# Moving the values of an attention core by one item, joining its softmax guards, and reordering the norm ahead of two mixers

## The reference

```python
def rmsnorm(x, g):
    y = xf * lax.rsqrt(jnp.mean(xf * xf, axis=-1, keepdims=True) + EPS)
    return (y * g.astype(jnp.float32)).astype(x.dtype)

def attend_block(qb, keys, values, masks, sink):
    ...
    m = sink_f
    for s in scores:
        m = jnp.maximum(m, jnp.max(s, axis=-1))
    denom = jnp.exp(sink_f - m)
    for s, vp in zip(scores, values):
        p = jnp.exp(s - m[..., None])
        denom = denom + jnp.sum(p, axis=-1)
        out = out + jnp.einsum('bkgqs,bskd->bqkgd', p.astype(vp.dtype), vp).astype(jnp.float32)
    out = out / jnp.moveaxis(denom, -1, 1)[..., None]
    ...

def fourier_mix(h, w):
    f = jnp.fft.fft2(hg, axes=(1, 3), norm='ortho').real
    return f.reshape(B, L, D).astype(h.dtype) @ w
```

## Time and profile before

| | before |
|---|---|
| median of 3 runs | 2664.11 us (2659.36 to 2665.26) |
| the profiled execution | 2665.53 us, its span 2663.7 us |
| TensorE matmuls busy | 2573.9 us, 97% of the span |
| VectorE busy | 1984.8 us, 75% |
| ScalarE busy | 1299.1 us, 49% |
| GpSimd busy | 115.5 us, 4% |
| mean granted TensorE clock | 0.984 of full |
| attention core of layer 0 | about 143 to 275 us |
| norm and pooling mixer | about 814 to 862 us |
| norm and start of the Fourier mixer | about 1328 to 1357 us |
| attention core of layer 3 | about 2014 to 2132 us |

### The profile page before, as it was taken

The page is one execution under the profiler, slowest core; times in us unless marked ns, Lnnn a source line. Parts: engine busy times, 40 slices in busy tenths (PEclk is TensorE's granted clock), DMA queues, the critical chain, the costliest instruction groups (busy, mean ns, idle before and its releaser), DMA issues.

```text
span 2663.7 us, 43103 instructions
## 1 busy us (share of the span) xinstructions
PE 2573.9 (97%) x15856; PEld 2383.5 (89%) x15856; DVE 1984.8 (75%) x3736; ACT 1299.1 (49%) x2291; POOL 115.5 (4%) x146
## 2 busy tenths in 40 slices
PE   6989999999998999999989999999998999999999
PEld 4966899999998999999879999999997699999998
DVE  3777488888896888888855888888868946754772
ACT  3467365425524663355244662454347936633551
POOL 2000100000012000000101000000100010000000
PEclk9999899999998999999989999999999999999999
DMA  7224122433341334434302335334320012222222
GB/s 292 64 95 148 58 101 104 163 138 118 108 168 48 103 110 160 154 105 146 124 21 72 116 111 184 111 110 153 118 71 29 2 56 72 78 87 64 76 83 78
DMA packets 72274, 279.64 MB, mean 105 GB/s; under 512 B 7888, under 2 KB 11344, under 8 KB 68560
## 3 DMA queue, kind: packets, MB, share of 16 engines
q1 hardware_dynamic: 72144, 277.93, 30.5%
HBM read 274.75 MB, written 3.15 MB: 104 GB/s over the span
## 4 chain that ended last, share of the span: by engine, by line
PE 89%; DVE 7%; issue 2%; ACT 1%; DMA 1%; POOL 0%; SPq 0%; DVEq 0%; ACTq 0%
PE ps L575 20%; PE ps L573 16%; PE ps L574 16%; PE ps L576 15%; PE ps L577 11%; PE ps L792 2%; PE ps L777 2%; PE ps L761 1%; PE ps L634 1%; DVE h L1406 1%; PE ps L687 1%; DVE prob L1609 1%; DVE ada_w L1352 1%; PE ps L828 1%; PE ps L569 1%
## 5 line engine op out<-in xcount | busy, mean ns | idle before, releaser
L575 PE MATMUL ps<-h,w_hi 128*128 128x512 f32 x1768 | 700.5, 396 | 0.0
L573 PE MATMUL ps<-h,w_hi 128*128 128x386 f32 x1768 | 604.8, 342 | 8.2 <-DVE h L1406 4.9
L574 PE MATMUL ps<-h,w_hi 128*128 128x386 f32 x1768 | 602.9, 341 | 0.0
L576 PE MATMUL ps<-h,w_lo 128*128 128x386 f32 x1768 | 598.7, 339 | 0.0
L950 ACT ACTIVATE tail<-ps 128x256 f32<-128x256 f32 x281 | 108.3, 386 | 966.0 <-PE ps L577 965.4
L577 PE MATMUL ps<-h,w_lo 128*128 128x256 f32 x1768 | 503.4, 285 | 0.0
L577 PEld LDWEIGHTS ps<-h,w_lo 128*128 128x128 f32 x1768 | 333.7, 189 | 79.6
L1293 DVE TENSOR_TENSOR w_lo<-w_raw,w_hi 128x1024 fp32r<-128x1024 f32 (+1 forms) x288 | 377.4, 1311 | 4.9 <-ACT w_hi L945 1.7
L573 PEld LDWEIGHTS ps<-h,w_hi 128*128 128x128 f32 x1768 | 339.3, 192 | 11.3 <-DVE h L1406 7.2
L574 PEld LDWEIGHTS ps<-h,w_hi 128*128 128x128 f32 x1768 | 335.8, 190 | 0.0
L575 PEld LDWEIGHTS ps<-h,w_hi 128*128 128x128 f32 x1768 | 334.0, 189 | 0.0
(11 more groups left out here) (166 smaller groups left out, 3890.0 us busy)
## 6 DMA issues: line engine op xcount, KB each, us to landing
w_raw<-in_w_in SPq DMA_DIRECT2D x176, 512.0 KB, 3.6
w_raw<-in_w_out SPq DMA_DIRECT2D x64, 704.0 KB, 4.1
ada_w<-in_ada_t SPq DMA_DIRECT2D x42, 1024.0 KB, 6.3
row_w<-in_ada_t SPq DMA_DIRECT2D x60, 512.0 KB, 3.5
ada_w<-in_ada_w SPq DMA_DIRECT2D x18, 1024.0 KB, 5.0
w_raw<-in_w_qkv SPq DMA_DIRECT2D x24, 512.0 KB, 3.5
w_raw<-in_w_o SPq DMA_DIRECT2D x16, 512.0 KB, 3.5
first_w<-in_ada_w SPq DMA_DIRECT2D x6, 1024.0 KB, 14.3
```

The costliest lines, as they stand in the source:

```text
L573: pe.matmul(main, wh, b[:, 0, 0:MAIN], start=first, stop=False)
L574: pe.matmul(main, wh, b[:, 1, 0:MAIN], start=False, stop=False)
L575: pe.matmul(wide, wh, b[:, :, MAIN:NT], start=first, stop=last, skip_group_check=True)
L576: pe.matmul(main, wl, b[:, 0, 0:MAIN], start=False, stop=last)
```

## The change

It has four edits.

1. In the attention core, `values(w)` comes one iteration later on TensorE (`values(w-3)`), with `out_hi` and `out_lo`; `probT` gets a third buffer. The loops run one iteration longer.
2. `masked` runs both heads' mask passes, then forms both guards with two instructions over both heads (a product and a minimum) in place of one two-scalar instruction for each head. `max_made` counts items in place of heads, so `exps(w)` waits for both heads' guards.
3. Ahead of the pooling and Fourier mixers GpSimd doesn't add the last square. TensorE sums `sq_sum` with six squares added, then, in the same accumulation, the last square by itself.
4. Ahead of the Fourier mixer the tables are split behind the root: four between the inversion and the copy into `rstd`, six after the first four tiles.

```diff
@@ gpsimd
-                        pool.tensor_tensor(sq_sum[:], sq_sum[:], sq[kk % 2][:], ALU.add).then_inc(sq_added, 1)
+                        if kk == KT - 1 and explicit(layer, second):
+                            pool.sem_inc(sq_added, 1)
+                        else:
+                            pool.tensor_tensor(sq_sum[:], sq_sum[:], sq[kk % 2][:], ALU.add).then_inc(sq_added, 1)
@@ tensor
-                pe.wait_ge(sq_added, (KT - 1) * (m + 1))
+                lone = explicit(layer, second)
+                pe.wait_ge(sq_added, (KT - 1) * (m + 1) - lone)
...
-                block_sums(sq_sum, ones[:], 1).then_inc(sum_done, 1)
+                if not lone:
+                    block_sums(sq_sum, ones[:], 1).then_inc(sum_done, 1)
+                    return
+                block_sums(sq_sum, ones[:], 1, last=False)
+                pe.wait_ge(sq_added, (KT - 1) * (m + 1))
+                block_sums(sq[(KT - 1) % 2], ones[:], 1, first=False).then_inc(sum_done, 1)
...
-                            pe.wait_ge(max_made, 2 * (w - 1))
+                            pe.wait_ge(max_made, w - 1)
...
-                        if w - w0 >= 2:
-                            values(w - 2)
+                        if w - w0 >= 3:
+                            values(w - 3)
@@ scalar
+                        act.wait_ge(max_made, w + 1)
                         for hd in range(2):
                             st = stat[:, w % 2, hd, :]
-                            act.wait_ge(max_made, 2 * w + hd + 1)
...
-                        if w - w0 >= 2:
-                            act.wait_ge(o_done, w - 1)
+                        if w - w0 >= 3:
+                            act.wait_ge(o_done, w - 2)
...
-                        if w - w0 >= 2:
-                            out_hi(w - 2)
+                        if w - w0 >= 3:
+                            out_hi(w - 3)
...
+                    high_tables(range(4))
                     shifted(layer, range(4))
-                    high_tables(range(8, 10))
+                    high_tables(range(4, 10))
...
-                if layer + 1 < DEPTH and KINDS[layer + 1] == "fnet":
-                    act.wait_ge(unit_done, UNIT0[layer + 1])
-                    high_tables(range(8))
@@ vector
                 if m:
                     invert(r, 1)
+                if KINDS[layer] == "fnet" and not second:
+                    split_tables(range(4))
                 dve.wait_ge(inv_turned, r + 1)
...
-                if kind == "fnet":
-                    split_tables(range(8))
...
-                    split_tables(range(8, 10))
+                    split_tables(range(4, 10))
...
-                            dve.tensor_scalar(st[:, 1:2], st[:, 0:1], neg_scale[:, tile, nb, hd:hd + 1],
-                                              neg_sink[:, a, head:head + 1],
-                                              ALU.mult, ALU.min).then_inc(max_made, 1)
+                        st, head = stat[:, w % 2, :, :], 8 * ga + r
+                        if w - w0 < KT:
+                            dve.wait_ge(q_scaled, KT * a + tile + 1)
+                        own.link(dve.tensor_tensor(st[:, :, 1], st[:, :, 0], neg_scale[:, tile, nb, :], ALU.mult))
+                        dve.tensor_tensor(st[:, :, 1], st[:, :, 1], neg_sink[:, a, head:head + 5:4],
+                                          ALU.min).then_inc(max_made, 1)
...
-                        if w - w0 >= 3:
-                            out_lo(w - 3)
+                        if w - w0 >= 4:
+                            out_lo(w - 4)
```

More of the change, by code:

```diff
@@ L627, in first_unit_tiles, with block_sums @@
                     first_tile(1, kk)
-            def block_sums(src, sel, cols):
+            def block_sums(src, sel, cols, first=True, last=True):
                 for tb in range(5):
@@ L633, in block_sums @@
                     c0 = SUMS.start + 2 * tb
-                    mm = pe.matmul(ps[:, INV_CTX, c0:c0 + cols], src[:, at:at + P], sel, start=True, stop=True)
+                    mm = pe.matmul(ps[:, INV_CTX, c0:c0 + cols], src[:, at:at + P], sel,
+                                   start=first and (last or tb == 0), stop=last, skip_group_check=first != last)
                 return mm
@@ L797, in _ @@
                     scores(w0)
-                    for w in range(w0, w0 + 42):
+                    for w in range(w0, w0 + 43):
                         if w + 1 < w0 + 40:
@@ L1410, in gained_low, with split_tables @@
                     op.then_inc(hl_made, 1)
+            def split_tables(rows):
+                for n in rows:
+                    dve.wait_ge(tabh_made, n + 1)
+                    dve.tensor_tensor(tab_lo[:, n, :], tab_raw[:, (n + 2) % 10, :], tab_hi[:, n, :].bitcast(F32),
+                                      ALU.subtract).then_inc(tabl_made, 1)
             def norm(layer, second, first=0):
@@ L1516, in _ @@
                 u0 = UNIT0[layer]
-                def split_tables(rows):
-                    for n in rows:
-                        dve.wait_ge(tabh_made, n + 1)
-                        dve.tensor_tensor(tab_lo[:, n, :], tab_raw[:, (n + 2) % 10, :], tab_hi[:, n, :].bitcast(F32),
-                                          ALU.subtract).then_inc(tabl_made, 1)
-                if kind == "fnet":
-                    split_tables(range(8))
                 norm(layer, False, KT if layer == 0 else 0 if explicit(layer, False) else KT - 1)
@@ L1612, in masked @@
                                 accum_out=st[:, 0:1]))
-                            head = 8 * ga + 4 * hd + r
-                            if w - w0 < KT and hd == 0:
-                                dve.wait_ge(q_scaled, KT * a + tile + 1)
-                            dve.tensor_scalar(st[:, 1:2], st[:, 0:1], neg_scale[:, tile, nb, hd:hd + 1],
-                                              neg_sink[:, a, head:head + 1],
-                                              ALU.mult, ALU.min).then_inc(max_made, 1)
+                        st, head = stat[:, w % 2, :, :], 8 * ga + r
[4 more added lines that the diff above has]
+                                          ALU.min).then_inc(max_made, 1)
                     def normed(w):
@@ L1635, in out_lo @@
                                           h_hi[:, tile, cols].bitcast(F32), ALU.subtract).then_inc(ol_made, 1)
-                    for w in range(w0, w0 + 43):
+                    for w in range(w0, w0 + 44):
                         if w < w0 + 40:
```

9 lines of the change are left out of this document (6 added, 3 removed).

## The result

The changed kernel takes 2649.7 us (median of 5 runs, 2648.4 to 2651.0), the kernel before, in runs on the same chip, 2661.7 us (5 runs, 2659.4 to 2665.3). The ratio is 0.995, with a 95% interval of 0.994 to 0.996: between 10 and 16 us faster. The forecast was 11.0 us, which from the median then known, 2664.1, gave 2653.1.

What follows compares the result with a forecast made beforehand. TensorE, busy for 97% of the span, was taken as the bound. Guard 4.2, later values 2.6, last square 2.8 and tables 1.4 sum to 11.0 us: from a median of 2664.1 to 2653.1 us, range 2648.5 to 2660.0.

Steps and rivals of the forecast that it cites:

- the four places named: Where TensorE idles or runs at its lower clock: layer 3's core, layer 0's core, both cores' ends, ahead of both mixers.
- Guard: VectorE in both attention cores: one pair of guard instructions for both heads saves 0.11 us an item.
- Rival 1: Both cores: the guard saves nothing, as two instructions with a wait cost the same; 6.8 us gained, 2657.3, chance 0.20.
- Guard, where it is paid: Layer 0's pairs 1.8 us, context items 0.9 in each core, layer 3's last five 384-key items 0.55; sum 4.2 us.
- Values later, start: Start of each core: the third iteration has no values, 0.8 us gained in each core, bounds 0 and 0.86.
- Values later, "0.5 us in each core" at the end: End of each core: last transposes no longer stand behind waiting values, 0.5 us gained in each, bounds 0 and 1.1.
- Last square: Norm before pooling: second five sums start sooner and run at high clock, root 2.8 us earlier, bounds 1.7 and 3.5.
- Rivals 2 and 3: 2: waits only move, guard saves nothing, 2.9 us, chance 0.11; 3: ScalarE late on second head, 2672.3 us, chance 0.05.
- the cover that the prediction put at 0.06 us: Steady items of layer 3's core: both heads' guards are ready 0.06 us before ScalarE begins its exponentials, costed at nothing.
- Fourier mixer: Norm before the Fourier mixer: tables behind the root, add removed; net 1.4 us gained, bounds 0.2 and 2.7.
- I keep 2.28 us for them: Before the Fourier mixer: the second sums start just behind the clock's fall and still take 2.28 us.
- the stall: Fourier mixer: stage_one(1) waits behind the six later splits; TensorE's stage_one(0) covers all but some 0.2 us.

Runs made afterwards that it cites:

- e3: The kernel before with only the guard of both heads in one pair of instructions; ratio 0.9998 (0.9990 to 1.0007) to the kernel before.
- e4: The kernel before with only the values one item later and the third buffer; ratio 0.9992 (0.9982 to 1.0002) to the kernel before.
- e8: The changed kernel with layer 0's last three items putting values into two banks by turns; ratio 0.9963 (0.9949 to 0.9977) to the kernel before.
- e14: e13 plus 12 unread products in each of the two gaps at the start of both cores; ratio 0.9937 (0.9923 to 0.9950) to the kernel before.
- e11: The kernel before, unchanged, for a second profile; ratio 1.0010 (0.9999 to 1.0020) against itself.
- e13: The changed kernel with e8's two banks and unread products in TensorE's gaps ahead of the mixers; ratio 0.9949 (0.9936 to 0.9963) to the kernel before.
- e17: e14 with the six later table splits moved behind the first stage-one results; 2643.3 us against 2662.5 for the kernel before, ratio 0.9926.

## Where the prediction held, and which steps of it failed

The total came out near the forecast of 11.0 us, and that is partly luck. Averaged over all profiles with the same code in a stretch (5 to 10 for each version), the gains are:

| stretch | before | changed | gain | forecast |
|---|---|---|---|---|
| layer 0 | 670.3 | 668.5 | 1.8 | 4.0 |
| pooling | 42.4 | 39.4 | 3.0 | 2.8 |
| Fourier mixer | 55.8 | 53.3 | 2.5 | 1.4 |
| layer 3 | 747.0 | 743.8 | 3.2 | 2.75 |

That is 10.5 us, and the timed gain of 10 to 16 us agrees. What layer 0 fell short by, 2.2 us, the Fourier mixer and layer 3 nearly made up. Layer 0's average is the least sure: profiles of one code lie up to 2.9 us apart there (667.9 to 670.8 with the changed cores), as the clock's low stretches fall. TensorE is the bound, and the gains lie in the four places named; but the step that failed is the end of layer 0's core, with the adding up of edits that depend on each other, and a term of the Fourier mixer was mis-sized.

- **Guard: right.** 0.10 us an item against 0.11 forecast. Rival 1 is out: the same 0.16 us instruction holds the next for 0.20 us with a wait behind it (2052.92 to 2053.12) and 0.08 without (2053.12 to 2053.20).
- **Guard, where it is paid: right only together with the later values.** I added the terms as if independent. e3 shows 0.5 us in layer 3 where the forecast had 1.45 for it; VectorE ran ahead and then waited for TensorE's scores.
- **Values later, start: right.** The first conditioning products follow the first scores by 16.68 and 17.09 us in the two profiles of after (17.65 and 17.62 before), and the later values alone gain 1.9 us in layer 3.
- **Values later, "0.5 us in each core" at the end: the step that failed, in layer 0.** The step counted what the last transposes no longer wait for and left out that one bank serves all values there, so that each waits for `out_lo` of the item before. The last values follow each other at 1.40 us, one more of them stands at the end, and the end grew by 0.8 us instead of shrinking by 0.5 (e4, with the later values alone, has it too: 7.48 us against 6.93). With two banks (e8) it is 1.9 to 2.3 us shorter than with one. That is 1.3 of the 2.2 us by which layer 0 fell short of its 4.0; what the rest is stays open.
- **Last square: right.** 2.8 forecast, 3.0 found. Rivals 2 and 3 did not occur. ScalarE does wait for the guard, 0.17 us in each of the last context items of layer 3 and, in one of the two profiles, up to 0.32 us in items 3 to 12, so the cover that the prediction put at 0.06 us is not always there; no loss by it is seen.
- **Fourier mixer: right mechanism, term mis-sized.** "I keep 2.28 us for them" is the term that was off. The sums took 1.28 us (1.0 us of gain), a little of the turn came with it (0.2), and the stall was 0.43 instead of 0.2. 1.4 became 2.5, inside the bound of 2.7. I had read the moment of the clock's fall from one profile as if it belonged to the code. The other 1.6 us of the pair's 4.1 is no gain: it is a stretch at the low clock that before's profile had and after's had not, and the second profiles show it the other way round.
- **Not seen at all:** that the Fourier edits gain 0.4 and 0.0 us without each other and 2.8 together (from the last unit to the first product), and that the splits' cover was TensorE's low clock (0.50 from 1323.0 to 1333.25 in after). With the clock up (e14) the same splits cost 1.98 us.

## What to carry to other kernels

When the chain of waits goes through a norm or another short serial stretch, look for a second chain just behind it before pricing an edit: two edits may be worth 0.4 and 0.0 us alone and 2.8 us together. Compare two profiles by the lengths of stretches with unchanged code as well; here those moved by up to 2.9 us, as much as the gains looked for. Ask also at the end of a pipelined loop which buffer every item shares: a shift that costs nothing in the middle can queue there. Where TensorE idles for microseconds ahead of dense work, useless products that fit into the gap are worth trying, sized from their own rows, and then the next cover that they remove has to be looked for.

## What the runs showed of the hardware

The moment at which TensorE's clock falls differs between executions of one kernel: before the Fourier mixer 2.1 or 5.0 us behind the last unit, at the end of layer 0's core 12 or 4 us ahead of the unit behind it (before and e11), and a later 3.4 us at the low clock comes or stays away. An fp32 product of 128 by 128 is two instructions and takes 0.23 us at full clock (e13's 16 behind pooling's turn: 32 instructions in 3.74 us at 1.00). With the gaps filled the mean granted clock rose from 0.985 (after) to 0.994 (e17), and the times of five runs lay within 1.6 us of each other. The same kernel with the sums late gave the same four lengths within 0.3 us in three profiles; three are too few to tell whether chance acts less on it.
